# Seven-product runs: the last up pair's work laid out over the run, and two of the seven additions per pair made as one of 512 columns

## The reference

```python
def sqrelu_mlp(h, w1, w2):
    a = jnp.square(jax.nn.relu(h @ w1))
    return a @ w2
...
        h = h + sqrelu_mlp(rmsnorm(h, mlp_norm[i]), mlp_w1[i], mlp_w2[i])
```

## Time and profile before

| | us |
|---|---|
| median of 3 runs | 2303.91 |
| lowest, highest | 2299.0, 2303.97 |
| the profiled execution's own time | 2297.27 |
| its span in the profile | 2294.8 |
| PE busy | 2230.2 (97%) |
| DVE busy | 1695.8 (74%) |
| ACT busy | 1075.9 (47%) |
| POOL busy | 448.9 (20%) |
| PE idle in front of a product, waiting for an add (`L1755`) | 28.6, nine times |

### The profile page before, as it was taken

The page is one execution under the profiler, slowest core; times in us unless marked ns, Lnnn a source line. Parts: engine busy times, 40 slices in busy tenths (PEclk is TensorE's granted clock), DMA queues, the critical chain, the costliest instruction groups (busy, mean ns, idle before and its releaser), DMA issues.

```text
span 2294.8 us, 31756 instructions
## 1 busy us (share of the span) xinstructions
PE 2230.2 (97%) x12018; PEld 1923.9 (84%) x12018; DVE 1695.8 (74%) x2601; ACT 1075.9 (47%) x1714; POOL 448.9 (20%) x330
## 2 busy tenths in 40 slices
PE   6999999999999999999999999999999999999999
PEld 5898779889788888888887788888888888888989
DVE  8965677857888876877657868884456667687788
ACT  4233443434477744443446736663344443544343
POOL 7402112313400040312330000002001004031234
PEclk9999999999999999999999999999999999999999
DMA  5573323233222223233232222124322222322323
GB/s 187 116 221 104 95 80 111 74 110 102 90 69 66 71 78 96 74 106 102 83 111 83 83 92 65 56 74 147 92 91 85 71 83 92 101 74 92 112 73 110
DMA packets 80165, 219.33 MB, mean 96 GB/s; under 512 B 18593, under 2 KB 28065, under 8 KB 79521
## 3 DMA queue, kind: packets, MB, share of 16 engines
q1 hardware_dynamic: 73568, 212.11, 29.6%
q10 hardware_dynamic: 6464, 5.47, 0.8%
HBM read 206.93 MB, written 6.29 MB: 93 GB/s over the span
## 4 chain that ended last, share of the span: by engine, by line
PE 67%; DVE 4%; ACT 1%; issue 1%; DVEq 0%; ACTq 0%
PE lin L617 16%; PE lin L619 16%; PE lin L618 16%; PE tr L804 2%; PE sc L804 2%; PE tr L805 2%; PE tr L806 2%; PE sc L805 2%; PE sc L806 2%; PE tr L892 1%; PE sc L1062 1%; PE tr L934 0%; PE tr L933 0%; PE sc L879 0%; PE sc L1063 0%
## 5 line engine op out<-in xcount | busy, mean ns | idle before, releaser
L617 PE MATMUL lin<-x_hi,w_hi 128*128 128x512 f32 x1472 | 580.8, 395 | 3.9 <-DVE w_lo L1784 2.2
L619 PE MATMUL lin<-x_hi,w_lo 128*128 128x512 f32 x1472 | 573.3, 390 | 0.0
L618 PE MATMUL lin<-x_lo,w_hi 128*128 128x512 f32 x1472 | 573.1, 389 | 0.0
L1229 ACT ACTIVATE w_hi<-w_raw 128x1024 fp32r<-128x1024 f32 x253 | 268.1, 1060 | 556.1 <-PE lin L619 540.8
L1784 DVE TENSOR_TENSOR w_lo<-w_raw,w_hi 128x1024 fp32r<-128x1024 f32 x253 | 329.6, 1303 | 91.8 <-ACT w_hi L1229 89.8
L617 PEld LDWEIGHTS lin<-x_hi,w_hi 128*128 128x128 f32 x1472 | 276.3, 188 | 66.7 <-DVE w_lo L1784 4.2
L619 PEld LDWEIGHTS lin<-x_hi,w_lo 128*128 128x128 f32 x1472 | 276.2, 188 | 58.0
L618 PEld LDWEIGHTS lin<-x_lo,w_hi 128*128 128x128 f32 x1472 | 276.5, 188 | 57.0 <-issue 1.2
L1205 ACT ACTIVATE w_hi<-w_raw 128x512 fp32r<-128x512 f32 (+1 forms) x231 | 149.0, 648 | 249.6 <-PE sc L806 82.0
L1735 DVE TENSOR_TENSOR w_lo<-w_raw,w_hi 128x512 fp32r<-128x512 f32 (+1 forms) x231 | 255.1, 1104 | 6.2 <-ACT w_hi L1205 6.2
L804 PE MATMUL sc<-hid_hi,w_hi 128*128 128x256 f32 x560 | 167.7, 300 | 29.0 <-DVE resid L1755 28.6
(11 more groups left out here) (520 smaller groups left out, 4611.8 us busy)
## 6 DMA issues: line engine op xcount, KB each, us to landing
w_raw<-w SPq DMA_DIRECT2D x353, 512.0 KB, 3.5
w_raw<-w_mem SPq DMA_DIRECT2D x16, 512.0 KB, 4.1
ssm_mt<-ssm_kp SPq DMA_DIRECT2D x64, 64.0 KB, 2.7
ssm_u<-x_a SPq DMA_DIRECT2D x1, 2048.0 KB, 10.8
kv_scratch<-mem_stage SPq DMA_DIRECT2D x8, 256.0 KB, 4.7
z_b<-z_scratch SPq DMA_DIRECT2D x4, 512.0 KB, 5.1
resid<-x_b SPq DMA_DIRECT2D x1, 2048.0 KB, 10.1
out<-resid SPq DMA_DIRECT2D x8, 256.0 KB, 3.7
```

What stands on the lines that cost most here:

```text
L617: nc.tensor.matmul(out, wh[:, w], xh[:, k, 0:cols], start=(k == 0), stop=False)
L618: nc.tensor.matmul(out, wh[:, w], xl[:, k, 0:cols], start=False, stop=False)
L619: last = nc.tensor.matmul(out, wl[:, w], xh[:, k, 0:cols], start=False, stop=(k == KC - 1))
L1229: nc.scalar.activation(WH[:, b, :], raw[:, r, :], ACT.Copy).then_inc(s_hi, 1)
```

## The change

Three edits in one, all in the MLP's runs.

1. Where a run follows directly on an up stage whose hidden values feed another run (`UNDER_RUN`, seven of the nine runs), what DVE has to do for that stage's last odd slab is no longer done ahead of add 0, but piece by piece between the run's adds and splits: sum A after product 0, B after 2, C after 3, raw low after 5, and left in two halves of 512 columns after 7 and 9. ACT's high part of the four sums moves behind the form made after product 5. In the two runs that follow up3 of mlp1 and mlp2 only the last slab's low part (there `lo` of `H3L`) is moved, to after product 5. In every run split 3 moves from ahead of add 0 to behind it.
2. Product 1 now goes to the left half, and products 3 and 5 to the right half, of one bank. There is no add 1; add 5 takes the whole bank, 512 columns. A pair has six adds.
3. In up stages, too, left is two `tensor_tensor` instructions of 512 columns where it was one `scalar_tensor_tensor` of 1024. Semaphore counts follow.

Also gone is PE's wait, ahead of down3 of mlp1 and mlp2, for the adds of all but the last pair.

```diff
-        PBANK = [[t[:, 0:L // 2] for t in SC], [t[:, 0:L // 2] for t in TR]]
+        PBANK = [[t[0][:, 0:L // 2], t[1][:, L // 2:L], t[1][:, 0:L // 2]] for t in (SC, TR)]
+        PWIDE = [t[1][:] for t in (SC, TR)]
         BANK_OF = [0, 2, 0, 1, 0, 1, 0]
...
-                pe.wait_ge(s_ev, r.prods + PRODS * p + (j - 1 if j != 4 else 3))
+                pe.wait_ge(s_ev, r.adds + ADDS * p + (1, 2, 3, 4)[(2, 4, 5, 6).index(j)])
...
-            def forms_hi(r):
+            def forms_hi(r, behind=None):
...
+                    if g == 5 and behind is not None:
+                        behind()
...
                 p, j = divmod(g, PRODS)
                 dve.wait_ge(s_prod, r.prods + g + 1)
-                dve.wait_ge(s_ev, r.prods + g)
+                if j == 1:
+                    return
+                dve.wait_ge(s_ev, r.adds + ADDS * p + SEEN[j])
...
+                if j == 5:
+                    out, bank = R[:, p % (KC // 2), :], PWIDE[p % 2]
                 TT(out, out, bank, op).then_inc(s_ev, 1)
 
-            def adds(r, left=None):
+            def adds(r, left=None, sums=None, raw_lo=None):
 
                 for g in range(r.n):
                     added(r, g)
-                    if 0 < g <= r.n - HALVES:
+                    if g <= r.n - HALVES:
                         form_lo(r, g + HALVES - 1)
...
-                    if g == 1 and left is not None:
-                        left()
+                    if sums is not None and g in (0, 2, 3):
+                        sums((0, 2, 3).index(g))
+                    if raw_lo is not None and g == 5:
+                        raw_lo()
+                    if left is not None and g in (7, 9):
+                        left((7, 9).index(g))
...
-                    for g in (2, 3):
-                        form_lo(RUN_AT[sl.at + 1], g)
+                    form_lo(RUN_AT[sl.at + 1], 2)
...
+                                def left(n, q=q, i=i):
+                                    f = slice(2 * n, 2 * n + 2)
+                                    if n == 0:
+                                        dve.wait_ge(s_h, c.up(s_h))
+                                    low = (HB_LO0, HB_LO1A)[q % 2][:, f, i, :]
+                                    TT(low, APS[:, f, :], f32(HB_HI[q % 2][:, f, i, :]), ALU.subtract).then_inc(s_hid, 1)
+                                    c.up(s_hid)
+                                if not (stage_name in UNDER_RUN and sl.idx == KC - 1):
+                                    for m in range(3):
+                                        sums(m)
+                                    raw_lo()
+                                    sums = raw_lo = None
```

More of the change, by code:

```diff
@@ L95 @@
 RUN_AT, RUN_BEFORE, RUN_OF = {}, {}, {}
-_forms = _prods = _sums = 0
+_forms = _prods = _sums = _adds = 0
 for _r in (Run(_s) for _s in RUNS):
-    _r.forms, _r.prods, _r.sums = _forms, _prods, _sums
+    _r.forms, _r.prods, _r.sums, _r.adds = _forms, _prods, _sums, _adds
     _forms += _r.n + (2 if _r.exits else 0)
@@ L101 @@
     _sums += 4 * _r.pairs
+    _adds += (PRODS - 1) * _r.pairs
     for _n in _r.stages:
@@ L104 @@
     RUN_AT[_r.first], RUN_BEFORE[_r.first - 2] = _r, _r
+UNDER_RUN = {f"{_m}.up{_q}" for _m in ("mlp1", "mlp2", "mlp3") for _q in (1, 2, 3)
+             if FIRST[f"{_m}.up{_q}"] + KC in RUN_AT and f"{_m}.down{_q}" in RUN_OF}
 def pair_slab(at):
@@ L589, in _ @@
             for p in range(KC // 2):
-                done = end.prods + PRODS * (end.pairs - KC // 2 + p)
-                for n, count in ((p, 6), (p + KC // 2, 7)):
+                done = end.adds + ADDS * (end.pairs - KC // 2 + p)
+                for n, count in ((p, 5), (p + KC // 2, 6)):
                     sp.wait_ge(s_ev, done + count)
@@ L826, in mlp @@
                         r = RUN_OF[f"{name}.down{q - 1}"]
-                        pe.wait_ge(s_ev, r.prods + r.n - PRODS)
                         stage(stage_name, H3H, H3L)
-                        pe.wait_ge(s_ev, r.prods + r.n)
+                        pe.wait_ge(s_ev, r.adds + ADDS * r.pairs)
                 hid_at[0] += hid_seen(QUARTERS - 1) if f"{name}.down3" in RUN_OF else hid_seen(QUARTERS - 2) + KC
@@ L1395, in mlp @@
             def mlp(name, next_gain, squares=False):
+                behind = None
                 for part in ("up0", "up1", "down0", "up2", "down1", "up3", "down2", "down3"):
@@ L1998, in mlp @@
             def mlp(name, next_gain):
-                left = None
+                left = sums = raw_lo = None
                 for part in ("up0", "up1", "down0", "up2", "down1", "up3", "down2", "down3"):
@@ L2005, in mlp @@
                         if RUN_OF[stage_name].stages[0] == stage_name:
-                            adds(RUN_OF[stage_name], left)
-                            left = None
+                            adds(RUN_OF[stage_name], left, sums, raw_lo)
+                            left = sums = raw_lo = None
                         continue
@@ L2021, in mlp @@
                             if left is not None:
-                                left()
+                                left(0)
+                                left(1)
                                 left = None
@@ L2036, in mlp, with sums @@
[L2036 to L2040, removed]
+                                def sums(n):
+                                    if n == 0:
+                                        b12 = TSQ[:, 1, :].unsqueeze(1).to_broadcast([P, 2, L // 2])
+                                        after(TT(APS[:, T1_:N3_ + 1, :], b12, TSQ[:, 0:4:3, :], ALU.subtract))
+                                    elif n == 1:
+                                        after(TT(APS[:, T2_, :], TSQ[:, 3, :], APS[:, T1_, :], ALU.subtract))
+                                    else:
+                                        TT(APS[:, N4_, :], TSQ[:, 2, :], APS[:, T2_, :], ALU.subtract).then_inc(s_hsum, 1)
@@ L2043, in mlp @@
                                 r = RUN_OF[f"{name}.down{q - 1}"]
-                                dve.wait_ge(s_ev, r.prods + r.n)
+                                dve.wait_ge(s_ev, r.adds + ADDS * r.pairs)
                             dve.wait_ge(s_evac, sl.done(-1))
```

37 lines of the change are left out of this document (23 added, 14 removed).

## The result

| | before | after |
|---|---|---|
| median, us | 2303.8 (2299.0 to 2303.97, 4 runs) | 2267.3 (2264.28 to 2269.03, 4 runs) |
| ratio | | 0.9845, 95% interval 0.9827 to 0.9863 |
| profiled execution, us | 2297.27 | 2269.03 |
| span, us | 2294.8 | 2267.3 |

A forecast was written before the change was run, and what follows sets the result against it. PE bounds the kernel, busy 97%; its runs lose 52.1 us (28.6 waits, 13.0 slow clock, 10.5 spread). With 19.8 left after the change, 32.3 us less gives 2270 us, range 2252 to 2286.

The forecast's parts named there:

- start wait: PE's wait ahead of product 2 for add 0: 3.62 us in seven runs, 1.60 in two, claimed to go.
- The clock comes back: Behind the long wait of seven runs PE ran at a reduced clock; the lost 13.0 us were to return whole.
- The sign that was named for it: In the 8 us after a run's start, granted clock 1.00 and 64 or more matmul starts.
- New waits: Moved DVE work meeting POOL additions early in seven runs: six PE waits, 2.76 us per run, longest 0.83.
- The walk: DVE's new queue stepped through the first run with trace durations, giving each product's lateness; 2.76 us per run together.
- The wide add takes the 0.41 us per later pair: From the third pair on, splits start ahead of POOL and 0.41 us per pair goes, some 9 us in all.
- Left in halves costs nothing: In up stages, 1.28 us of DVE in place of 1.22, where DVE waits for PE anyway: no cost.
- ACT's part is hidden: ACT's 1.06 us for the sums' high part hides behind product 9's form, made by 347.7; otherwise 1 us per run.
- A: Rival: the new waits vanish as POOL and DVE fall into another rhythm; 2252 to 2260 us, chance 0.13.
- B: Rival: new waits are larger or bring the clock down, giving back 13.0 us; 2283 us, chance 0.16.
- C: Rival: add 0 waits for ACT's late square, some 1 us per run remains; gain near 25 us, chance 0.05.
- D: Rival: POOL and DVE saturate what they share, delay passes from pair to pair; slower, 2328 us, chance 0.04.

The follow-up runs named there:

- filler: Kernel before, with 28 matmuls of unused result added on PE between products 1 and 2 of the seven long-wait runs; 2282.27 us against 2297.69.
- run 1: No follow-up kernel: the first of the nine MLP product runs inside each execution; 47.50 us in the kernel before, 43.43 in the changed one.
- left whole: Changed kernel with left as one instruction of 1024 columns behind product 7, nothing behind product 9; one execution, 2265.49 us.
- wide only: Kernel before with only the one-bank 512-column add for products 1, 3 and 5, DVE's other order kept; 2285.23 us against 2297.69.
- spread only: Kernel before with only the last up pair's work moved, seven adds of 256 columns kept in the old banks; 2272.38 us against 2297.69.
- late in run: Changed kernel with the moved pieces in the last pair of 28-product runs, and at other places in the 56-product run; 2251.37 us against 2297.69.
- short POOL: Changed kernel with POOL's four sums per pair cut to 128 of 512 columns; one execution, 2244.78 us, against 2298.28 for the kernel before.
- raw low moved: Kernel before with only raw low moved from ahead of add 0 to behind add 1; one execution, 2287.86 us.

## Why the prediction was right

The mechanism was right: two costs that end with the start wait, and a smaller one that the moved work brings back. In the runs the gain came out 2.6 us smaller than reckoned, mostly in the new waits. That the whole time is yet so close, 2267.3 against 2270, is in part luck: the medians moved by 6.8 us more than the runs did.

- **The start wait goes.** It did, in all nine runs. DVE did add 0 at 341.59, product 2 began at 342.23 and not a tenth late:

```profile
341.59 0.42 DVE L1775 TENSOR_TENSOR resid<-resid,sc 128x256 f32<-128x256 f32 x1
341.93 0.68 DVE L1751 TENSOR_TENSOR w_lo<-t,w_hi 128x512 fp32r<-128x512 f32 x1
342.53 0.68 DVE L2063 TENSOR_TENSOR acc_psq<-t_sq 128x512 f32<-128x512 f32 x1
343.25 1.67 DVE L1751 TENSOR_TENSOR w_lo<-w_raw,w_hi 128x512 fp32r<-128x512 f32 x1
344.84 0.41 DVE L1775 TENSOR_TENSOR resid<-resid,sc 128x256 f32<-128x256 f32 x1
345.17 1.44 DVE L1751 TENSOR_TENSOR w_lo<-w_raw,w_hi 128x512 fp32r<-128x512 f32 x1
```

- **The clock comes back, 13.0 us.** Shown by the filler at 12.8. This term, some two fifths of the gain in the runs, stands in no list of waits; it was read from the starts per window. The sign that was named for it, clock 1.00 and 64 or more starts in the 8 us after a run's start, came true in its first half only: in run 1 the clock is 1.00 and there are 60 starts (342.23 to 350.23), because the new waits take their share.
- **New waits, 2.76 us per run.** The step was right in kind and place, and too small: 3.1 us (43.42 less the floor of 40.31). The rows above show the first of it, beside these of POOL:

```profile
342.78 1.58 POOL L2680 TENSOR_TENSOR t<-w_raw 128x512 f32<-128x512 f32 x1 [2.78 <-DVE w_lo L1751]
344.44 1.62 POOL L2682 TENSOR_TENSOR w_raw<-w_raw 128x512 f32<-128x512 f32 x1
```

  Split 4 meets POOL and takes 1.67 us, split 5 takes 1.44, and what follows is late. The walk had 0.13, 0.57, 0.75, 0.34 and 0.83 us ahead of products 4, 5, 9, 11 and 12; measured are 0.29, 0.72, 0.68, 0.29 and 0.86. It missed that DVE began `L2041` 0.65 us later than in run 1 before, held up by the halves of left (see left whole). It also missed that the product behind a late one comes another 0.07 us late: products 6, 10 and 13 start 1.51 us after the one ahead and not 1.44. Over the nine runs: 22.3 us measured (425.58 - 403.30), 19.8 reckoned.
- **The wide add takes the 0.41 us per later pair.** Right in kind: in wide only, later pairs take 10.08 us. On top of the moved work it gives 6.0 us, where "some 9 us in all" had been said; alone it gives 9.0. The 0.41 was charged to every pair from the third on. In spread only, the third pair of run 1 loses 0.39, of which 0.30 goes with the wide add; the last pair, in which POOL makes no more sums, loses only 0.07. The full change's own time doesn't hang on this, since the walk took these pairs as free. (The matmuls of the earlier trace rows at 372.74 and 374.18 begin products 20 and 21, not 19 and 20; the 1.44 us between them stand.)
- **Left in halves costs nothing.** Wrong by 0.4 us per run. The up stages themselves are no longer, since the stages between the runs kept their 1499.4 us: the reason given, that DVE waits for PE there anyway, holds up to the last slab. Behind that, DVE comes late into the run.
- **ACT's part is hidden.** It was, but the time given for it was not right. The form for product 9 needs POOL's third sum; its high part was made from 350.80, not by 347.7, and that of the four sums behind it, to 352.38. The half of left that needs it began at 354.44.
- **The sum.** 32.3 us reckoned, 29.7 measured in the runs. The medians differ by 36.5. The profiled executions differ by 28.2: 2297.27 is below every run of the kernel before in the table above, and 2269.03 is the highest of the changed one; the rest is most likely the scatter of the first 340 us and of the length of the slow stretches before, which only one profile of each kernel shows.
- **The rivals.** A (no new waits) is what late in run and short POOL approach, so it was a real alternative, but not with this placement. B's fall of the clock under several short waits did not come: the clock is 1.00 in all nine runs with 21 waits of 0.5 to 0.6 us. (The price of B gives 2283; the 2286 of the range is not worked out in the text.) What the Trainium skill tells of short idle times ("TensorE: Matmul & The Clock Gate", A second HAM failure mode) no run here shows. C and D did not happen: no debt passed beyond the second pair.
- **The price of the slow clock.** The rule of the Trainium skill ("TensorE: Matmul & The Clock Gate", Terms) gave about 1 us more than the starts for all seven runs; the filler's 12.8 us agree with the starts.

## What to carry to other kernels

When PE waits, read the starts of its matmuls behind the wait as well: of some 5.5 us that a start wait of 3.6 cost here, nearly two were slow clock (12.8 / 7), and with the wait cut from 3.6 to 3.0 us the clock still fell every time. When work is moved off a critical point, look for a place where the engine that it contends with is at rest; with the same six instructions of DVE a run loses 3.1 us when they stand beside POOL's additions and 0.6 when they stand behind them. Look also at the stage ahead of that point: cutting one instruction of 1.22 us in two let an addition in between and made DVE 0.65 us late where it counted. A queue walked with durations from the trace, blocked time included, came within 0.5 us per 43 us run.

## What was not expected of the hardware

The time up to the first run moves by 10 us between executions, with the clock at 0.83 or 1.00 between 120 and 180 us. PE's longest idle time in that stretch is 1.00 us in the profile before and 0.95 in that of wide only, so no long wait, like those in the runs, brought it down. Two profiles with a longer one, 1.18 us in spread only and 1.20 in short POOL, kept the clock at 1.00. What decides it stays open; no run here was made to tell.

Nearer the start of the program the same profiles say something on idle times between those of the runs, of which 1.60 us left the clock up and 3.02 brought it down. Around 45 us PE idles for a time that differs between executions. Where its longest idle time there is 1.35, 1.42, 1.70 or 1.77 us (spread only, short POOL, wide only, late in run), the granted clock over the first 60 us, as far as it is recorded, is 1.00. Where it is 2.15 us (before), 2.35 (filler) or 2.53 (full change, raw low moved, left whole), the clock goes to half beside it, and the same mean is 0.94, 0.97, and 0.92, 0.97 and 0.92. PE's matmuls around that place are other and smaller ones than in the runs, so this is an observation and no measured limit.
